# Sample-state updates of two heads in one slot, with their decays moved ahead, in a hybrid S5 and DeltaNet decoder layer

## The reference

```python
g_last = g_i[..., -1:]
S = (S * jnp.exp(g_last)[..., None]
     + jnp.einsum('bhcd,bhce->bhde', k_i * jnp.exp(g_last - g_i)[..., None], v_new))
```

## Time and profile before

| what | value |
|---|---|
| median of 3 runs | 1994.21 us (1993.83 to 1995.47) |
| profiled execution, its own time | 1993.93 us |
| its span | 1992.2 us |
| PE busy | 1975.6 us (99%) |
| DVE busy | 1127.6 us (57%) |
| ACT busy | 813.3 us (41%) |
| Pool busy | 303.5 us (15%) |
| granted PE clock | 0.999 of full speed |
| HBM traffic over the span | 155 GB/s |

### The profile page before, as it was taken

The page is one execution under the profiler, slowest core; times in us unless marked ns, Lnnn a source line. Parts: engine busy times, 40 slices in busy tenths (PEclk is TensorE's granted clock), DMA queues, the critical chain, the costliest instruction groups (busy, mean ns, idle before and its releaser), DMA issues.

```text
span 1992.2 us, 38789 instructions
## 1 busy us (share of the span) xinstructions
PE 1975.6 (99%) x15613; PEld 1936.8 (97%) x15613; DVE 1127.6 (57%) x1409; ACT 813.3 (41%) x1068; POOL 303.5 (15%) x382
## 2 busy tenths in 40 slices
PE   9999999999999999999999999999999999999998
PEld 8999999899999889999999999999999999999997
DVE  7799997873645677544444444434444444444554
ACT  7343336733434553344333333333333333334543
POOL 4956443000002110011000000000000000001111
PEclk9999999999999999999999999999999999999999
DMA  9544445544437586644544444444444444444442
GB/s 229 180 138 129 132 133 155 162 124 140 120 112 210 163 279 223 221 150 139 158 148 147 148 149 150 151 149 157 148 147 148 149 151 148 148 142 158 143 148 101
DMA packets 300837, 310.16 MB, mean 156 GB/s; under 512 B 25013, under 2 KB 290886, under 8 KB 300466
## 3 DMA queue, kind: packets, MB, share of 16 engines
q1 hardware_dynamic: 296800, 296.76, 48.4%
q0 software_dynamic: 3504, 11.64, 2.0%
q10 hardware_dynamic: 418, 0.12, 0.0%
HBM read 291.34 MB, written 17.14 MB: 155 GB/s over the span
## 4 chain that ended last, share of the span: by engine, by line
PE 93%; DVE 4%; DMA 1%; ACT 1%; issue 1%; ACTq 0%; SPq 0%; DVEq 0%
PE pg L2157 86%; DVE cacc L1742 2%; DVE wlo L1404 1%; PE side_a L2199 1%; PE side_a L2190 1%; DMA raw<-in_w_out 1%; PE side_a L2502 0%; ACT whi L957 0%; PE side_a L2157 0%; DMA par2n<-in_conv_w 0%; PE side_a L2521 0%; PE side_b L2157 0%; PE side_b L2190 0%; PE side_a L2421 0%; PE side_b L2421 0%
## 5 line engine op out<-in xcount | busy, mean ns | idle before, releaser
L1404 DVE TENSOR_TENSOR wlo<-raw,whi 128x1024 fp32r<-128x1024 f32 (+1 forms) x528 | 650.6, 1239 | 642.5 <-ACT whi L957 640.9
L957 ACT ACTIVATE whi<-raw 128x1024 fp32r<-128x1024 f32 (+1 forms) x528 | 545.1, 1039 | 907.0 <-PE pg L2157 839.9
L2157 PE MATMUL pg<-xhi,whi 128*128 128x320 f32 x2816 | 478.3, 312 | 1.4 <-ACT whi L957 1.4
L2157 PE MATMUL pg<-xhi,wlo 128*128 128x320 f32 x2816 | 470.7, 309 | 1.2 <-DVE wlo L1404 1.2
L2157 PE MATMUL pg<-xlo,whi 128*128 128x320 f32 x2816 | 470.3, 309 | 1.1 <-DVE xlo L1411 1.1
L2157 PEld LDWEIGHTS pg<-xhi,whi 128*128 128x128 f32 x2816 | 424.4, 188 | 10.6 <-issue 6.8
L2157 PEld LDWEIGHTS pg<-xhi,wlo 128*128 128x128 f32 x2816 | 427.4, 188 | 2.4 <-DVE wlo L1404 2.2
L2157 PEld LDWEIGHTS pg<-xlo,whi 128*128 128x128 f32 x2816 | 427.4, 188 | 1.4 <-DVE xlo L1411 1.4
L927 POOL TENSOR_TENSOR fsi<-fsg,inv 128x640 f32<-128x640 f32 x22 | 43.3, 1969 | 706.6 <-ACT fsg L1287 706.6
L2157 PE MATMUL pg<-mhi,wlo 128*128 128x320 f32 x704 | 118.9, 309 | 0.0
L2157 PE MATMUL pg<-mhi,whi 128*128 128x320 f32 x704 | 118.8, 309 | 0.0
(11 more groups left out here) (488 smaller groups left out, 1698.2 us busy)
## 6 DMA issues: line engine op xcount, KB each, us to landing
raw<-in_w_in SPq DMA_DIRECT2D x144, 512.0 KB, 4.1
raw<-in_w_gate SPq DMA_DIRECT2D x88, 512.0 KB, 3.5
raw<-in_w_up SPq DMA_DIRECT2D x88, 512.0 KB, 3.5
raw<-in_w_down SPq DMA_DIRECT2D x80, 512.0 KB, 3.5
raw<-in_w_out SPq DMA_DIRECT2D x32, 512.0 KB, 3.5
raw<-in_w_ple_gate SPq DMA_DIRECT2D x32, 512.0 KB, 3.5
raw<-in_w_a SPq DMA_DIRECT2D x16, 512.0 KB, 5.2
raw<-in_w_b SPq DMA_DIRECT2D x16, 512.0 KB, 4.3
```

Source lines behind the costliest of these rows:

```text
L957: act.activation(whi[:, r, 0:nk, :], raw[:, r, 0:nk, :], ACT.Copy).then_inc(w_hi, 1)
L1404: dve.tensor_tensor(wlo[:, r, 0:nk, :], raw[:, r, 0:nk, :], whi[:, r, 0:nk, :].bitcast(F32), ALU.subtract).then_inc(w_lo, 1)
L2157: ins = pe.matmul(out[:, m, 0:N], w[:, r, k, m * P:(m + 1) * P], a[:, k0 + k, :], start=first and k == 0 and part == 0, stop=last and k == ...
```

## The change

Two heads share a slot of two units, four slots in place of eight. So that both heads' products use different row groups, the odd head's masked values stand in the rows 64 to 127 of `vnb`, and ACT copies the odd heads' keys to the rows 64 to 127 of `ktok` once, at `m1` (2, 2). ACT makes the masked values of two heads at `o` 2. The multiplication of the first four heads' states by the decay is done on DVE in the slots `vn` 2 and `o` 2. Pool's tables get one more power in `tb` (17 entries), and are made by products alone: each step multiplies the finished powers 1 to m by the top power.

```diff
@@ -204,8 +204,8 @@
             slot([("o", c), ("s", c)], 1)
         else:
             slot([("o", c)], 1)
-            for i in range(H):
-                slot([("su", i)], 1)
+            for i in range(0, H, 2):
+                slot([("su", i), ("su", i + 1)], 2)
     slot([("ona", 0)], 1)
     for j in range(H // 2):
         slot([("on", j)] + [("ona", j + 1)] * (j + 1 < H // 2), 2)
@@ -347,7 +347,7 @@
         ct = z5.take("ct", [P, 2, K5, P])
         ct_end = z5.at
         k0 = z5.take("k0", [P, K5, 32])
-        tb = z5.take("tb", [P, 2, NT, 16])
+        tb = z5.take("tb", [P, 2, NT, 17])
         ta = z5.take("ta", [P, 2, NT, PCK // 16])
         h0s = z5.take("h0s", [P, 2, NT, NB])
         a0 = z5.take("a0", [P, 2, NT, NB])
@@ -419,7 +419,7 @@
 
         zst = Zone(nc, zq_at, 4 * 4096)
         st_ring = [zst.take("st2", [P, NB, P]), zst.take("st3", [P, NB, P])]
-        vnb = zst.take("vnb", [NSM, 4, NB // 2, P])
+        vnb = zst.take("vnb", [P, 4, NB // 2, P])
         zst2 = Zone(nc, zq_at + 2 * H * NPAD * 4, H * NPAD * 4)
         st_ring = [zst2.take("st0", [P, NB, P]), zst2.take("st1", [P, NB, P])] + st_ring
 
@@ -496,6 +496,10 @@
 
         def drain(ins, key):
             ins.then_inc(drained[fill_at[key][0]], 1)
+
+        def sample_rows(i):
+
+            return slice(NSM * (i % 2), NSM * (i % 2) + NSM)
 
         def heads(t, c):
 
@@ -743,21 +747,15 @@
                 o.step(pool.memset(t[:, 1, :, 0:1], 0.0))
                 o.step(pool.tensor_copy(t[:, 0, :, 1:2], sr.unsqueeze(2)))
                 o.link(pool.tensor_copy(t[:, 1, :, 1:2], si.unsqueeze(2)))
-                w = sc5w
-                cur, n = (sr, si), 2
-                while True:
-                    k = n.bit_length() % 2
-                    nxt = (w[:, 2 * k, :], w[:, 2 * k + 1, :])
-                    square(nxt[0], nxt[1], cur[0], cur[1], [w[:, 4 + e, :] for e in range(3)])
-                    cur = nxt
-                    if n == size:
-                        return cur
-
-                    def bc(v):
-                        return v.unsqueeze(2).broadcast_to([P, NT, n])
-                    product(t[:, 0, :, n:2 * n], t[:, 1, :, n:2 * n], t[:, 0, :, 0:n], t[:, 1, :, 0:n],
-                            bc(cur[0]), bc(cur[1]), pt5[:, 0, :].rearrange("p (t n) -> p t n", n=8)[:, :, 0:n],
-                            pt5[:, 1, :].rearrange("p (t n) -> p t n", n=8)[:, :, 0:n])
+                n = 1
+                while n < size - 1:
+                    m = min(n, size - 1 - n)
+
+                    def top(r):
+                        return t[:, r, :, n:n + 1].broadcast_to([P, NT, m])
+                    product(t[:, 0, :, n + 1:n + 1 + m], t[:, 1, :, n + 1:n + 1 + m], t[:, 0, :, 1:1 + m], t[:, 1, :, 1:1 + m],
+                            top(0), top(1), pt5[:, 0, :].rearrange("p (t n) -> p t n", n=8)[:, :, 0:m],
+                            pt5[:, 1, :].rearrange("p (t n) -> p t n", n=8)[:, :, 0:m])
                     n *= 2
 
             def tables():
@@ -766,10 +764,8 @@
                 w = [sc5w[:, k, :] for k in range(12)]
                 square(w[8], w[9], sp5[:, 1, :], sp5[:, 2, :], w[4:7])
                 square(w[10], w[11], sp5[:, 3, :], sp5[:, 4, :], w[4:7])
-                cur = powers(tb, 16, w[8], w[9])
-                o.step(pool.tensor_copy(w[8], cur[0]))
-                o.link(pool.tensor_copy(w[9], cur[1]))
-                powers(ta, PCK // 16, w[8], w[9])
+                powers(tb, 17, w[8], w[9])
+                powers(ta, PCK // 16, tb[:, 0, :, 16], tb[:, 1, :, 16])
 
             def h0_terms():
 
@@ -791,8 +787,8 @@
                 shape = [P, 2, PCK // 16, 16]
                 ar = ta[:, 0, 2 * hq:2 * hq + 2, :].unsqueeze(3).broadcast_to(shape)
                 ai = ta[:, 1, 2 * hq:2 * hq + 2, :].unsqueeze(3).broadcast_to(shape)
-                br = tb[:, 0, 2 * hq:2 * hq + 2, :].unsqueeze(2).broadcast_to(shape)
-                bi = tb[:, 1, 2 * hq:2 * hq + 2, :].unsqueeze(2).broadcast_to(shape)
+                br = tb[:, 0, 2 * hq:2 * hq + 2, 0:16].unsqueeze(2).broadcast_to(shape)
+                bi = tb[:, 1, 2 * hq:2 * hq + 2, 0:16].unsqueeze(2).broadcast_to(shape)
 
                 def v(t):
                     return t.rearrange("p t (a b) -> p t a b", b=16)
@@ -1186,6 +1182,9 @@
                             copy(full[BLOCK[b], :, BLOCK[b]], tmt[BLOCK[b]]).then_inc(sem("corners_copied"), 1)
                     else:
                         drain(act.activation(hsplit(m1[0:n]), blocks_of(key)[0:n], ACT.Copy), key)
+                    if (c, k) == (2, 2):
+                        act.wait_ge(sem("kd_ready"), 3)
+                        copy(ktok[NSM:P, 1:H:2, :], ktok[0:NSM, 1:H:2, :]).then_inc(sem("kd_doubled"), 1)
                 elif what == "vn":
                     c = a[0]
                     n = CHUNKS[c][1]
@@ -1200,13 +1199,14 @@
                     if a[0] == 2:
                         wait_drained(act, ("vn", 2))
                         masked_values(0)
+                        masked_values(1)
                 elif what == "sq":
                     if a[0] == 0:
                         wait_filled(act, ("s", 1))
                     wait_filled(act, key)
                     copy(vn[NSM:P, a[0], :], ps(key)[NSM:P, 0, 0:P]).then_inc(sem("qs_ready"), 1)
-                elif what == "su" and a[0] + 1 < H:
-                    masked_values(a[0] + 1)
+                elif what == "su" and a[0] + 2 < H:
+                    masked_values(a[0] + 2)
                 elif what == "ysplit":
                     act.wait_ge(multiplied, pair_first[pair_of["gate", 15]] + 2)
                     act.wait_ge(sem("gelu_done"), K5)
@@ -1232,7 +1232,7 @@
                 if i >= 4:
                     wait_filled(act, ("su", i - 4))
                 for j in range(NB // 2):
-                    ins = copy(vnb[:, i % 4, j, :], vn[0:NSM, (i + 4) % H, :], scale=seqm[:, j:j + 1])
+                    ins = copy(vnb[sample_rows(i), i % 4, j, :], vn[0:NSM, (i + 4) % H, :], scale=seqm[:, j:j + 1])
                     o.step(ins) if j < NB // 2 - 1 else ins.then_inc(sem("vnb_ready"), 1)
 
             def last_states(hq):
@@ -1646,6 +1646,14 @@
                 n = CHUNKS[c][1]
                 m = lvl[0:n, k, 0:SB].unsqueeze(1).broadcast_to([n, H, SB])
                 dve.tensor_tensor(ltm[0:n], lt[0:n], m, ALU.mult).then_inc(sem("ltm_ready"), 1)
+
+            def scale_state(i):
+
+                if i < 4:
+                    wait_filled(dve, ("sq", i + 4))
+                dve.wait_ge(sem(f"st_landed_{i % 4}"), 16 * (2 if i < 4 else 3))
+                h, st = (i + 4) % H, st_ring[i % 4]
+                o.step(dve.tensor_tensor(st[:], st[:], egl[:, h, :].unsqueeze(2).broadcast_to([P, NB, P]), ALU.mult))
 
             def side(key):
                 what, a = key[0], key[1:]
@@ -1899,11 +1907,15 @@
                             o.step(ins) if h < H - 1 else drain(ins, key)
                 elif what == "su":
                     i = a[0]
-                    h, st = (i + 4) % H, st_ring[i % 4]
-                    dve.wait_ge(sem(f"st_landed_{i % 4}"), 16 * (2 if i < 4 else 3))
-                    o.link(dve.tensor_tensor(st[:], st[:], egl[:, h, :].unsqueeze(2).broadcast_to([P, NB, P]), ALU.mult))
+                    st = st_ring[i % 4]
+                    if i >= 4:
+                        scale_state(i)
+                    o.settle()
                     wait_filled(dve, key)
                     drain(dve.tensor_tensor(hsplit(st[:]), hsplit(st[:]), ps(key)[:].rearrange("p k (b e) -> p k b e", b=4), ALU.add), key)
+                elif what in ("vn", "o") and a[0] == 2:
+                    for i in ((0, 1) if what == "vn" else (2, 3)):
+                        scale_state(i)
                 elif what == "ysplit":
                     for k in range(0, K5, UK):
                         t = slice(k, k + UK)
@@ -2472,10 +2484,12 @@
                 elif what == "su":
                     i = a[0]
                     pe.wait_ge(sem("kd_ready"), 3)
+                    pe.wait_ge(sem("kd_doubled"), 1)
                     pe.wait_ge(sem("vnb_ready"), i + 1)
                     out = begin(key)
                     for k in range(2):
-                        rows = slice(NSM // 2 * k, NSM // 2 * (k + 1))
+                        at = sample_rows(i).start + NSM // 2 * k
+                        rows = slice(at, at + NSM // 2)
                         ins = pe.matmul(out[:, k, :], ktok[rows, (i + 4) % H, :],
                                         vnb[rows, i % 4].rearrange("j b e -> j (b e)"), start=True, stop=True)
                     end(ins, key)
```

## The result

The changed kernel takes 2000.77 us, the median of 7 runs (1998.65 to 2003.78). The kernel before, on the same chip, takes 1994.26 us, the median of 7 runs (1993.83 to 1995.47). The ratio is 1.0035 with a 95% interval from 1.0026 to 1.0044. The change is slower by 6.5 us; I had forecast 1993.3 us, and the result lies outside the range I gave, on the side to which I had given a chance of 0.05. The profiled execution of the changed kernel takes 2000.36 us with a span of 1998.3, against 1993.93 and 1992.2 before, so 6.43 us are to be found.

The account below looks back on a forecast made before the run. PE was taken as the bound, with 93% of the chain of waits. Gains of 0.2 and 0.8 us in the update halves, less 0.1 for weight loads, gave 1993.0; plus 0.28 for the median, 1993.3 us; range 1990.5 to 1995.8.

Parts of the forecast that it names:

- The step that failed: Pool's tables, early stage: even 20 us saved on Pool would change the total by 0, as PE sets the pace.
- The pair on PE: Update slots: two heads' products run side by side on PE's row groups, taking 1.08 us for a pair.
- The order of starts: Update slots: matmuls starting strictly in program order would delay each second head 0.53 us, taking 2.1 us from the best case.
- First and second hold: First slot's second unit waits 0.67 us for DVE's evacuation; then the second pair's hold for DVE's additions costs 2.24 us.
- Third hold: Fourth update slot: the sixth head's state, loaded behind the third head's store, comes late and holds PE 1.7 us.
- The slower rival: End of the updates: extra weight traffic delays the last head's state on DVE; about 1995.0 us, chance 0.12.
- The full gain: Update slots: regions are free in time and all 5.57 us are kept, giving 1988.6 us; chance 0.10.
- the two row groups of a pair might run in turn: Update slots: row groups work in turn, costing 2 x 0.53 us where no hold covers it; 1994.4 us, chance 0.05.
- the bound of 0.3 us on the stretch before 678: Sign of error: the prediction is wrong if the stretch before the updates moves by more than 0.3 us.
- Decays: Slots of vn 2 and o 2: four multiplications of 1.25 us fit DVE's idle time there, cost 0.
- copy of keys: ACT's copy in the slot of m1 (2, 2): hidden by 3.24 us idle soon after, cost 0, otherwise 0.6 us.

Follow-up runs that it names:

- e1: The kernel before with only Pool's new power tables added: 1998.92 us, ratio 1.0023.
- e2: The kernel before with the new tables, Pool's 256-column products waiting for both halves of DVE's twelve products: 1995.01 us, ratio 1.0005.
- e7: The changed kernel with the old tables and the first four heads' decays back in the update slots: 2000.35 us, ratio 1.0030.
- e6: The changed kernel with old tables, DVE's additions for the first four heads moved right behind the slot's last subtraction: 1993.2 us, ratio 0.9996.
- e3: The changed kernel with the old tables, so pairs and early decays only: 1996.46 us, ratio 1.0011.
- e9: The changed kernel plus Pool's wait for both halves of DVE's twelve products and early additions for the first four heads: 1993.96 us, ratio 0.9999.
- e4: The kernel before, one head per slot and old tables, with only the first four decays moved ahead: 1993.68 us, ratio 0.9995.
- e8: The changed kernel with old tables, without stores of the first four heads' states; later loads wait for the addition alone: 1993.0 us, ratio 0.9991.
- e5: The kernel before with the new tables, Pool's wide products waiting only for DVE's first six products: 1997.03 us, ratio 1.0012.

## Why the prediction was wrong, point by point

**The step that failed** is the one on Pool's tables: "PE sets the pace of that stage, so 0 either way". It asked who waits for Pool's results, and for that question 0 is right. DVE's wait of 2.27 us did not reach PE: from 85 to 123 us e1 stays 4.54 us behind the kernel before and gains nothing. The step did not ask what Pool's next products would run beside once they came 13 us earlier. That cost 4.4 us at the median (e1), 3.9 of which go with one wait (e2). The rows for it were in the profile of before. DVE's products take 0.69 to 0.74 us beside a squaring (68.12 to 70.93) and 0.79 to 0.91 beside Pool's products of 128 columns (72.11 to 77.21, the first of them below), and DVE's subtraction at 70.96 ended only 0.3 us ahead of PE's need at 72.49.

```profile
72.11 0.91 DVE L1576 TENSOR_TENSOR ctl<-ct,sp 128x512 f32<-128x512 f32 x1
```

The stretching itself was priced in no term. In the changed kernel six of DVE's products take 1.08 us each by starts (67.64 to 74.09), and three of Pool's 1.08 too (70.36 to 73.59). Without the other engine beside them DVE's take 0.68 (e2, 72.58 to 76.68); Pool's take 0.70 in the kernel before (88.59 to 90.69), where DVE is idle or in one short instruction. The Trainium skill (SBUF — State Buffer, Who interferes with whom) states that a DVE instruction with two inputs in SBUF contends with a GpSimd (Pool) instruction that reads SBUF, and that the port pair they share is an exclusive lock. The trace agrees that they disturb each other, and both go at one pace. Strict turns by whole instructions would take 0.68 + 0.70 = 1.38 us, an estimate from the rows above, and 1.08 is measured. So the two do not exclude each other for all of their time.

**The pair on PE, 1.08 us: right.** The third pair starts at 702.48 and 702.50 and its unit at 703.55, 1.07 us later. The row groups run side by side where nothing holds one of the fills. The order of starts that might have taken 2.1 us cost nothing: the four records begin at 702.48, 702.50, 703.02 and 703.03. In the first pair side_b came 0.34 us late, and the unit 1.40 behind the start instead of 1.08; that term was short by 0.3. ACT ended the masked values of the second head at 682.90, 0.1 us after the pair's start.

**First and second hold: right in place and near in size.** The hold of the second unit is 0.74 us by the starts (684.21 to 688.47, less 3.52), and 0.67 was worked out. The second pair's fills start at 688.4 and 689.6, and 688.2 and 689.4 were worked out; DVE's second addition starts at 692.84, so 688.2, as laid out. The third pair comes at 697.84, and 697.70 was worked out. e7 and e6 show the cause from both sides.

**Third hold: right cause, too small.** The load is asked for at 697.56 by that clock (697.2 worked out) and takes 8.6 us instead of 7.9. The unit behind the fourth pair starts at 709.86, not 708.8: 1.1 us more. As a hold it is 2.6 us where 1.7 was worked out. I had kept that end open ("if it lands late, the gain is eaten one for one").

**What follows a hold: not in the sum.** From 714.50 to 718.48 two passes of eight products take 3.98 us; the same two take 2.45 at 703.55. The lower clock costs 1.5 us there and 1.7 at 77 us. The forecast of 37.7 us for the stage, plus 1.1, plus 1.5, gives 40.3; measured are 40.36. Before the change there was nothing of it in these stretches, and I had written holds as if they cost only what they last. How often it comes is not shown: it stands in the one execution of the changed kernel that was profiled, and not in that of e3.

**Rivals.** The slower rival named the weights that follow the updates. In the changed kernel PE never gets there early enough for it to matter; in e6 and e9 it does, and 2.0 of 3.3 us and 1.7 of 3.2 are taken back. The full gain needed DVE's additions to end by 687.1; they end at 689.4 by that clock. In e6 they do end at 687.1, and then late weights and DVE's queue take 2.0 us back. That the two row groups of a pair might run in turn is refuted by the third pair. No rival stood for a loss outside the update stage; the bound of 0.3 us on the stretch before 678 was given as a sign of error, and it was missed by 4.3.

**Decays and copy of keys: right.** e4 gives 0.63 us in the stage, at the one hold that it removes; the 0.85 in the median is no more than the measurement can tell from nothing. The copy costs nothing that shows: between 128 and 678 us the distance to the kernel before changes by +0.20 us in e3, -0.15 in e6, +0.14 in e7 and -0.08 in e8.

## What to carry to other kernels

When work on a side engine gets faster, its successors move too: look up what they will run beside, not only who waits for them. A product of 256 columns on GpSimd beside one of 512 on VectorE cost each of them here half as much again (1.08 us against 0.70 and 0.68), so put the wider ones where VectorE has slack, with a wait if need be. A hold of TensorE can cost twice, once for itself and once for the slower clock behind it, so price that before counting a gain that leaves new holds. And where the DMA share is full, a faster TensorE may only reach the next late transfer sooner.

## What the runs showed of the hardware that was not expected

- The granted clock fell to its lower level for about 3.4 us after PE had waited 2.02 us (in the changed kernel and in e1), after 2.66 us at the start of the changed kernel, and after 1.53 us behind a short product. In e7 it fell for longer behind waits of 2.07 and 1.26 close together. It did not fall after waits of 1.39 and 1.45 us in e5, 1.33 in e3 and 1.77 in e6, nor after 1.94 at the start of e3. The two falls that I summed cost 1.5 and 1.7 us.
- The length of a wait does not settle it. Near the end of the program PE waits 1.68 us for DVE in all eleven kernels, behind the same work. In the profiled executions of the changed kernel, e1, e3, e5, e6 and e8 the clock falls while PE works on behind it; in those of the kernel before, e2, e4, e7 and e9 it does not. So a hold may bring the lower clock in one execution and not in another. Falls of this kind in some runs would be of the size of e3's spread of 4.6 us, but only one execution of each kernel was profiled, so that is not shown.
- The same 512-column product of DVE took 0.69 us alone and 1.00 to 1.21 us beside Pool's 256-column products. A TENSOR_SCALAR with one tensor as input was stretched too: four of them took 2.19, 2.49 and 3.33 us in three kernels.
- The records of a pair whose fills start together come as two of side_a, two of side_b, two of side_a, two of side_b. When the second fill is held, the first shows as one row of four. The two forms tell at a glance whether a pair went together or nearly so; in the first pair the second fill is 0.34 us late and the form is still the first.
